# First head of each mixer layer: the first half of the key weights moved between the two halves of the queries, and the last residual's squares put into other PSUM banks

## The chip, the cores and the metric

The kernel runs on one core of a Trainium2 chip. The metric is the device time of one execution in microseconds (us). Everything is computed in float32; the large matmuls run as three float32r products of a high and a low part of each operand.

## The reference, cut to what matters

One block of one kind (sparse attention, an LRU branch, a gated feed-forward) is followed by two layers of another kind. The change touches the start and the end of those two layers and the very end of the program.

```python
def second_block(x, norm1_g, w_in, q_norm_g, k_norm_g, ...):       # x: 1 x 512 x 1024
    for i in range(DEPTH_2):                                       # two layers
        xn = rmsnorm(x, norm1_g[i])
        proj = xn @ w_in[i]
        u_pool, q, k, v, g_a, g_b = jnp.split(proj, splits, axis=-1)
        q = q.reshape(b, s, DIFF_HEADS, 2, DIFF_QK_DIM).transpose(0, 2, 3, 1, 4)   # 4 heads
        k = k.reshape(b, s, DIFF_HEADS, 2, DIFF_QK_DIM).transpose(0, 2, 3, 1, 4)
        q = apply_partial_rotary(rmsnorm(q, q_norm_g[i]), cos, sin)
        k = apply_partial_rotary(rmsnorm(k, k_norm_g[i]), cos, sin)
        ...
        o = diff_attention(q, k, v, lam)
        ...
        x = x + merged @ w_out[i]
        hn = rmsnorm(x, norm2_g[i])
        gate, up = jnp.split(hn @ w_ffn_in[i], 2, axis=-1)
        x = x + (jax.nn.silu(gate) * up) @ w_ffn_out[i]
    return x
```

## The kernel before

x is kept transposed in `xT`, as 8 tiles of 128 channels by 512 tokens. A norm is not applied to x: `residual` writes x times the gain as a high and a low part into `xg`, squares go into PSUM (ScalarE, L2664) and are summed into `acc` (VectorE, L1628), and the projections run on `xg` before the norm's factor is known. The factor is put in later, when the products are read out of PSUM.

Each engine has its own program, in the order in which it is written; engines wait for one another by semaphores. The two mixer layers run in a loop on every engine. Weights come by DMA into four slots, are split into a high part (ScalarE, L3125, or GpSimd, L804) and a low part (VectorE, L2329, or GpSimd, L806) and go to one of three slots for TensorE, in the order of the chunk numbers that `mixer_order` gives out. The first three chunks of a layer are split by GpSimd at the end of the layer ahead.

PSUM has eight banks: `psA` (2), `psB` (5, of which `psS` is the first two and `psT` the other three) and `psO` (1). Projections go through a ring of four banks: `psA[0]`, `psA[1]`, `psT[1]`, `psT[2]`. The queries of a head take the first two of a layer (`TILE2` 0 and 1), its keys the other two.

A head's queries or keys are 256 columns wide and are made by `rows(x, n, j)` (L1471): for one half j of the contraction, 4 slices of 128 channels by 4 token blocks by 3 products, that is 48 matmuls of 128x256. The halves j = 0 and 1 are accumulated in the same banks. TensorE's order at the start of a layer is

- queries half 0, queries half 1 (the last of its slices waits for the last residual tile),
- the norm's sums: a 128x512 matmul with `ones` (L1518), a small one for the layer's lambda (L1520) and four of one column (L1522), which give each token's sum of squares,
- keys half 0, two slices of keys half 1, the transposes of the first half of the tokens of the queries (`rows_transposes`, L1511), the other two slices of keys half 1, half of `u0`, the transposes of the queries' second half, and so on to the values.

Between the sums and the first transposes VectorE makes the token factors (`token_scale`, L2307 to L2313), ScalarE squares the queries with them (`squares2`, L3132), VectorE sums the squares (L2333), ScalarE takes the roots (L3137, L3139), and VectorE applies them and the rotation (`rows_apply`, L2345 to L2363) and starts the norm's own factor (L1633). The first transposes wait for the rotation and, since they write `psO`, for L1633.

At the end of a layer `down_residual` (L2218, L2220) adds the last products to x and calls `residual` for the next layer's norm. After the second layer TensorE transposes x back (L1592), ScalarE copies it out of PSUM (L3292) and sends it to memory, in four blocks of tokens.

Of the kernel before, what the change touches and what calls it, by code (L numbers as in the profile page):

```python
# [17 lines left out]
ALU = mybir.AluOpType  # L18
ACT = mybir.ActivationFunctionType
AX = mybir.AxisListType  # L20

P = 128
# [46 lines left out]
def mixer_order():  # L69

    head = [("q", 0), ("q", 1), ("k", 0), ("k", 1)]
    units = [(x, 0, j) for x, j in head] + [("u", 0), ("u", 1), ("v", 0, 0), ("v", 0, 1)]
    for n in range(HEADS2 - 1):
        units += [(x, n + 1, j) for x, j in head]
        units += [("u", 2 * n + 2), ("p", n), ("u", 2 * n + 3), ("v", n + 1, 0), ("v", n + 1, 1)]
    units += [("g", 0, 0), ("g", 0, 1), ("p", HEADS2 - 1)]
    return units + [("g", m, x) for m in range(1, KT) for x in range(2)]
# [131 lines left out]
def build(nc, a, out):  # L209
    with ExitStack() as ctx:  # L210
# [19 lines left out]
        xT = keep(KT, T)  # L230
# [356 lines left out]
        def _(sp):  # L587
# [157 lines left out]
            with sp.Fori(0, LAYERS) as l:  # L745
                def col2(w, col, k0=0, kts=KT, each=KT):
                    h = kts // 2
                    return [(b, e, w[:, bass.ds(l * each + (k0 + b), e - b), bass.ds(col, P)]) for b, e in ((0, h), (h, kts))]

                c0 = l * C_LAYER + C_B2  # L750
                def head_rows(slot, b):
                    return slot.rearrange("p k n -> p (k n)").rearrange("p (k n) -> p k n", n=V2)[:, 2 * b:2 * b + 2, :]

                def head(x, n, j):
                    c = CHUNK2[x, n, j]
                    col = D * ("uqkv".index(x)) + n * V2
                    load(c0 + c, c % RAW, [(b, 0, wi2[:, bass.ds(l * KT + (4 * j + 2 * b), 2), col:col + V2]) for b in range(2)], head_rows, settle=True)

                def columns(key, col):
                    c = CHUNK2[key]  # L760
                    load(c0 + c, c % RAW, col2(wi2, col), settle=True)

                def pool_weights(g):
                    c = CHUNK2["p", g]
                    load(c0 + c, c % RAW, [(2 * k, 2 * k + 2, pw2[:, bass.ds(l * 8 + (g * 2 + k), 1), :, :].squeeze(1)) for k in range(2)], settle=True)

                def query_key(n):
                    for x in "qk":
                        for j in range(2):
                            head(x, n, j)  # L770

                query_key(0)
                for m in range(2):
                    columns(("u", m), m * P)
                for j in range(2):
                    head("v", 0, j)
                for n in range(HEADS2 - 1):
                    query_key(n + 1)
                    columns(("u", 2 * n + 2), (2 * n + 2) * P)
                    pool_weights(n)  # L780
                    columns(("u", 2 * n + 3), (2 * n + 3) * P)
                    for j in range(2):
                        head("v", n + 1, j)
                for m in range(KT):
                    for x in range(2):
                        columns(("g", m, x), m * P + D * (4 + x))
                    if m == 0:
                        pool_weights(HEADS2 - 1)
                tail(sp, load, stage, c0 + L_WO, lambda: sp.wait_ge(m2_dve.sem, m2_dve.at(l * KT + KT - 1)), lambda m: col2(wo2, m),
                     lambda x, b, q: gate_up2[:, b, bass.ds(l * KT // 2, KT // 2), x * DFF + 2 * q * P:x * DFF + (2 * q + 2) * P],  # L790
                     lambda r, m: col2(wd2, m, r, min(KT, FT - r), FT))
# [412 lines left out]
        def _(pe):  # L1204
# [233 lines left out]
            with pe.Fori(0, LAYERS) as l:  # L1438
# [17 lines left out]
                def rows(x, n, j, kts=range(4), ready=None):  # L1456

                    c, t = CHUNK2[x, n, j], TILE2[x, n]
                    if kts[0] == 0:
                        weights(c)  # L1460
                        if j == 0:
                            take(t)
                            take(t + 1)
                    w = slots2[c % 3]
                    for k in kts:
                        kt = 4 * j + k
                        if ready is not None:
                            ready(kt)
                        for q in range(TT):
                            for m, (xh, wh) in enumerate(((0, 0), (0, 1), (1, 0))):  # L1470
                                i = mm(ring(t + q // 2)[:, q % 2 * V2:(q % 2 + 1) * V2], xg[:, xh, kt, q * P:(q + 1) * P],  # L1471
                                       w[:, wh, k * V2:(k + 1) * V2], start=kt == 0 and q % 2 == 0 and m == 0,
                                       stop=kt == KT - 1 and q % 2 == 1 and m == 2, skip_group_check=True)
                    if kts[-1] == 3:
                        i.then_inc(used.sem, 1)
# [37 lines left out]

                ready = split_by(res_dve, l * 16 + 16)
                rows("q", 0, 0, ready=ready)
                rows("q", 0, 1, ready=ready)
                pe.wait_ge(res_dve.sem, res_dve.at(l * 16 + 23))
                mm(psO[:, :], ones, acc[:, :], start=True, stop=True)  # L1518
# [2 lines left out]
                for t in range(TT):  # L1521
                    i = mm(psT[:, 0, 8 + t:9 + t], acc[:, t * P:(t + 1) * P], ones[:, 0:1], start=True, stop=True)  # L1522
                i.then_inc(nm_pe.sem, 1)
                rows("k", 0, 0)
                rows("k", 0, 1, (0, 1))
                rows_transposes(0, "q", 0)
                rows("k", 0, 1, (2, 3))
# [60 lines left out]
            for t in range(TT):  # L1588
                if t >= 2:
                    pe.wait_ge(ou_act.sem, ou_act.at(t - 2))  # L1590
                for f in range(KT):
                    i = nc.tensor.transpose((psT, psS)[t % 2][:, f // 4, f % 4 * P:(f % 4 + 1) * P], xT[:, f, t * P:(t + 1) * P], ident)  # L1592
                i.then_inc(ou_pe.sem, 1)


# [1 line left out]
        def _(dve):  # L1597
# [14 lines left out]
            def flat(b):  # L1612
                return b[:, :, :, :].rearrange("p h k t -> p h (k t)")

            def residual(n, m, s, gain, add, c=None):

                x = xT[:, :, :].rearrange("p k t -> p (k t)")[:, bass.ds(m * T, T)]
                g2 = flat(xg)
                if add:
                    dve.wait_ge(used.sem, used.at(c))  # L1620
                    v.tensor_tensor(x, x, psA[:, s, :], ALU.add).then_inc(drained.sem, 1)
                dve.wait_ge(res_act.sem, res_act.at(n, "hi"))
                v.scalar_tensor_tensor(g2[:, 1, bass.ds(m * T, T)], x, gain, hi_f(g2[:, 0, bass.ds(m * T, T)]),
                                       ALU.mult, ALU.subtract).then_inc(res_dve.sem, 1)
                if add is False and n:
                    dve.wait_ge(res_dve.sem, res_dve.at(n - 1))
                dve.wait_ge(res_act.sem, res_act.at(n, "square"))
                v.tensor_tensor(acc[:, :], acc[:, :], psT[:, 1 + s, :], ALU.add).then_inc(res_dve.sem, 1)  # L1628

            def norm(k):  # L1630

# [470 lines left out]
            def tail_dve(c0, t0, k, n, of, gain1):  # L2102
# [112 lines left out]
                def down_residual(m):  # L2215
                    s = m % 2
                    dve.wait_ge(used.sem, used.at(c2 + (3 * m + 2)))
                    v.scalar_tensor_tensor(psA[:, s, :], psA[:, s, :], -0.5, c_rs[:, :], ALU.mult, ALU.mult).then_inc(dn_dve.sem, 1)  # L2218
                    dve.wait_ge(dn_dve.sem, dn_dve.at(d0 + m))
                    v.tensor_tensor(xT[:, m, :], xT[:, m, :], psA[:, s, :], ALU.add).then_inc(drained.sem, 1)  # L2220
                    residual(n + 8 + m, m, s, gain1(m), None)

                g, x0, d0, f0, p0 = of(QUADS), of(KT // 2), of(KT), of(QUADS - 1), of(5 * QUADS - 2)
                c2 = c1 + SEVEN * QUADS
# [412 lines left out]
        def _(act):  # L2637
# [18 lines left out]
                act.wait_ge(of.sem, of.at(n, "root"))  # L2656
                ac(n_r2[:, 0:w], n_r0[:, 0:w], ACT.Square, scale=dim ** -0.5).then_inc(of.sem, 1)

            def residual(n, t, m, s, gain):

                x = xT[:, :, :].rearrange("p k t -> p (k t)")[:, bass.ds(m * T, T)]
                act.wait_ge(drained.sem, drained.at(t))
                ac(flat(xg)[:, 0, bass.ds(m * T, T)], x, ACT.Copy, scale=gain).then_inc(res_act.sem, 1)
                ac(psT[:, 1 + s, :], x, ACT.Square).then_inc(res_act.sem, 1)  # L2664

            def norm(k, load=True):
                if load:
# [312 lines left out]
            def tail_act(c0, r0, t0, k, n, g, x0, loads, gain2, gain1):  # L2980
# [128 lines left out]
                for m in range(KT):  # L3109
                    if m < KT - 1:  # L3110
                        down_hi(3 * m + 3)
                        down_hi(3 * m + 4)
                        down_hi(3 * m + 5)
                    residual(n + 8 + m, t0 + 8 + m, m, m % 2, gain1(m))

            tail_act(C_WO, R_WO // RAW, T_WO, 1, 8, 0, 0, lambda q: (q // 2 + 1) * 64, lambda m: col("n2", m), lambda m: par2[:, bass.ds(m + PAR2["n1"].start, 1)])

# [171 lines left out]

            for t in range(TT):  # L3290
                act.wait_ge(ou_pe.sem, ou_pe.at(t))
                ac(yout[:, t, :], (psT, psS)[t % 2][:, 0:2, :].rearrange("p b d -> p (b d)"), ACT.Copy).then_inc(ou_act.sem, 1)  # L3292
                act.wait_ge(ou_act.sem, ou_act.at(t))
                act.dma_start(out[0, t * P:(t + 1) * P, :], yout[:, t, :]).then_inc(stored, 16)
            act.wait_ge(stored, TT * 16)
# [14 lines left out]
```

## Time and profile before

| | us |
|---|---|
| median of 3 runs | 2557.98 |
| lowest and highest run | 2553.32, 2561.17 |
| the profiled execution | 2563.48 |
| its span | 2560.7 |
| TensorE busy in it | 2491.8 (97%) |
| VectorE, ScalarE, GpSimd busy | 1614.1, 1358.4, 710.0 |
| mean granted TensorE clock | 0.984 of full |

A profiled execution is one execution, and all times of single instructions come from it. Its span is the time from the first instruction to the last; 2.8 us of its time lie around the span. A wait of TensorE is a wait of the kernel wherever TensorE has no spare time later, and at 97% it has little.

### The profile page before, as it was taken

The numbers are of one execution on the slowest core, as the hardware profiler recorded it, in microseconds if no ns is written. First come the engines' busy times: TensorE is split into PE (matmuls) and PEld (weight loads), VectorE is DVE, ScalarE is ACT, GpSimd is POOL, SyncE is SP. The second block draws the span as 40 slices with busy tenths as digits, with TensorE's granted clock in tenths as the row PEclk, the third lists the DMA queues.
The fourth block names the chain that finished last, engine by engine and source line by source line (L and its number), as shares of the span: only waits on it lengthen the run. The fifth ranks groups of instructions, "written<-read, shape, count | busy, mean of one in ns | idle before, by whom it ended". The sixth has DMA issues, their size and how long they took to land.

```text
span 2560.7 us, 42520 instructions
## 1 busy us (share of the span) xinstructions
PE 2491.8 (97%) x15323; PEld 2227.9 (87%) x15323; DVE 1614.1 (63%) x2680; ACT 1358.4 (53%) x2001; POOL 710.0 (28%) x373
## 2 busy tenths in 40 slices
PE   7999999999999999999999999999999999999998
PEld 6789988887889998899888899988898888899987
DVE  6567766664575664377775765673577766765653
ACT  4456664764377772244444576652344444667732
POOL 4335530000047760200000177720200000477600
PEclk9989998999999999999999999999999999999999
DMA  7321113333323323322223333333222233233232
GB/s 158 103 53 34 36 34 89 89 85 90 108 81 121 109 79 107 95 71 71 71 79 91 99 100 100 100 99 99 84 76 74 61 89 105 77 104 122 85 99 70
DMA packets 352569, 223.89 MB, mean 87 GB/s; under 512 B 57392, under 2 KB 350572, under 8 KB 352364
## 3 DMA queue, kind: packets, MB, share of 16 engines
q1 hardware_dynamic: 349404, 218.02, 29.2%
q10 hardware_dynamic: 2960, 3.22, 0.4%
q8 instruction: 119, 1.95, 0.3%
q14 instruction: 86, 0.70, 0.1%
HBM read 212.86 MB, written 2.10 MB: 84 GB/s over the span
## 4 chain that ended last, share of the span: by engine, by line
PE 82%; DVE 10%; ACT 4%; issue 3%; DMA 0%; DVEq 0%; ACTq 0%; POOL 0%
PE psA L1215 17%; PE psA L989 13%; PE psB L1238 13%; PE psA L1238 10%; PE psB L989 10%; PE psA L1471 6%; PE psB L1471 5%; PE psO L1116 3%; PE psB L1097 2%; PE psB L1073 1%; DVE b L2329 1%; DVE b L2213 1%; DVE b L2477 1%; DVE b L2159 0%; DVE b L1837 0%
## 5 line engine op out<-in xcount | busy, mean ns | idle before, releaser
L1215 PE MATMUL psA<-b,b 128*128 128x512 f32 x2448 | 568.5, 393 | 2.8 <-DVE b L1657 1.2
L1215 PEld LDWEIGHTS psA<-b,b 128*128 128x128 f32 x2448 | 460.1, 188 | 108.6 <-issue 4.1
L989 PE MATMUL psA<-b,b 128*128 128x256 f32 x3168 | 399.1, 284 | 10.1 <-DVE b L2159 5.0
L989 PEld LDWEIGHTS psA<-b,b 128*128 128x128 f32 x3168 | 387.4, 192 | 14.4 <-issue 8.8
L1238 PE MATMUL psB<-b,b 128*128 128x512 f32 (+4 forms) x1626 | 368.1, 384 | 7.7 <-DVE b L2046 4.5
L916 POOL TENSOR_TENSOR b<-b 128x1024 f32<-128x1024 f32 x33 | 80.6, 2442 | 1036.2 <-DMA b<-in_w_ffn_in 727.9
L1238 PEld LDWEIGHTS psB<-b,b 128*128 128x128 f32 (+2 forms) x1626 | 299.7, 196 | 68.3 <-DVE b L2046 4.9
L1238 PE MATMUL psA<-b,b 128*128 128x512 f32 x1356 | 325.9, 395 | 0.0
L3032 ACT ACTIVATE b<-b 128x1024 fp32r<-128x1024 f32 x231 | 244.2, 1057 | 137.9 <-PE psB L989 76.5
L1238 PEld LDWEIGHTS psA<-b,b 128*128 128x128 f32 x1356 | 253.7, 189 | 54.8 <-issue 1.0
L989 PE MATMUL psB<-b,b 128*128 128x256 f32 x2376 | 299.0, 282 | 0.0
L989 PEld LDWEIGHTS psB<-b,b 128*128 128x128 f32 x2376 | 290.3, 191 | 0.0
L2159 DVE TENSOR_TENSOR b<-psB,b 128x1024 fp32r<-128x1024 f32 x159 | 194.4, 1223 | 113.7 <-ACT psB L3039 113.4
L2145 DVE TENSOR_TENSOR b<-b,b 128x1024 fp32r<-128x1024 f32 x72 | 87.9, 1225 | 149.4 <-ACT b L3018 149.4
L940 POOL TENSOR_TENSOR b<-b,b 128x1024 fp32r<-128x1024 f32 x63 | 154.3, 2449 | 74.7 <-ACT b L3032 64.8
L3039 ACT ACTIVATE psB<-b 128x1024 f32<-128x1024 f32 x159 | 161.2, 1014 | 8.1 <-DVE b L2159 8.0
L3018 ACT ACTIVATE b<-b 128x1024 fp32r<-128x1024 f32 x72 | 76.3, 1059 | 167.2 <-PE psA L1215 164.7
L1471 PE MATMUL psA<-b,b 128*128 128x256 f32 x1152 | 148.6, 288 | 3.2 <-DVE b L2220 3.2
L1471 PEld LDWEIGHTS psA<-b,b 128*128 128x128 f32 x1152 | 143.6, 194 | 6.7 <-issue 6.0
L1471 PE MATMUL psB<-b,b 128*128 128x256 f32 x1152 | 147.8, 288 | 0.6 <-DVE b L2329 0.6
L1471 PEld LDWEIGHTS psB<-b,b 128*128 128x128 f32 x1152 | 143.2, 194 | 2.7 <-issue 2.4
L3125 ACT ACTIVATE b<-b 128x1024 fp32r<-128x1024 f32 x102 | 106.3, 1058 | 56.4 <-PE psA L1238 30.6
(318 smaller groups left out, 3393.8 us busy)
## 6 DMA issues: line engine op xcount, KB each, us to landing
b<-in_w_in SPq DMA_DIRECT2D x296, 256.0 KB, 3.0
b<-in_w_ffn_in SPq DMA_DIRECT2D x88, 512.0 KB, 5.9
b<-in_w_ffn_out SPq DMA_DIRECT2D x64, 256.0 KB, 3.0
b<-in_w_out SPq DMA_DIRECT2D x48, 256.0 KB, 2.9
b<-in_w_gate SPq DMA_DIRECT2D x22, 512.0 KB, 4.9
b<-in_w_up SPq DMA_DIRECT2D x22, 512.0 KB, 6.5
b<-in_w_down SPq DMA_DIRECT2D x32, 256.0 KB, 3.2
b<-in_w_ffn_out SPq DMA_DIRECT2D x32, 192.0 KB, 2.5
```

The lines of the kernel that those rows point to most:

```text
L916: nc.gpsimd.tensor_tensor(sum1[:, :], raw[:, 2, :], raw[:, 3, :], ALU.add).then_inc(sa_pool.sem, 1)
L940: nc.gpsimd.tensor_tensor(w[:, 1], quad_raw(q)[:, {A12: 1, A22: 3}[x]], hi_f(w[:, 0]), ALU.subtract).then_inc(w_lo.sem, 1)
L989: i = nc.tensor.matmul(banks[x][:, p * half_t:(p + 1) * half_t], w[:, wh, at:at + P], rhs[x][:, xh, j, :], start=first and j == 0 and p == ...
L1116: i = mm(psO[:, qt * P:(qt + 1) * P], PT[:, h, at:at + P], vtok[:, br, kt, n // 4, hd, :, :].rearrange("p h d -> p (h d)"), start=h == 0 a ...
L1215: i = mm(dst, w[:, wh, kt * P:(kt + 1) * P], rhs(xh, kt), start=first and kt == 0 and n == 0, stop=last and kt == kts - 1 and n == 2)
L1238: i = mm(dst, lh(x), rh(y), start=start and n == 0, stop=stop and n == 2, skip_group_check=skip)
L1471: i = mm(ring(t + q // 2)[:, q % 2 * V2:(q % 2 + 1) * V2], xg[:, xh, kt, q * P:(q + 1) * P], w[:, wh, k * V2:(k + 1) * V2], start=kt == 0 ...
L2145: v.tensor_tensor(w[:, 1], wraw[:, d % RAW], hi_f(w[:, 0]), ALU.subtract).then_inc(w_lo.sem, 1)
L2159: v.tensor_tensor(w[:, 1], src, hi_f(w[:, 0]), ALU.subtract).then_inc(w_lo.sem, 1)
L3032: ac(quad_slot(c)[:, 0], src[:, :], ACT.Copy).then_inc(w_hi.sem, 1)
L3039: ac(psS[:, :, :].rearrange("p b t -> p (b t)"), src[:, :], ACT.Copy).then_inc(wc_act.sem, 1)
L3125: ac(w[:, 0], wraw[:, c % RAW], ACT.Copy).then_inc(w_hi.sem, 1)
```

## The change

1. The first head's chunks stand in the order queries half 0, keys half 0, queries half 1, keys half 1, in `mixer_order` (chunk numbers, so weights' slots), in the DMA queue's program and in TensorE's program. The heads after the first keep theirs. TensorE makes the norm's sums after queries half 1, as before.
2. Keys half 0 now writes `psT[1]` and `psT[2]` before the last residual's squares have been read. So the last residual of a layer puts its squares into `psS`. The other residuals stay.
3. The squares of the second layer's last residual now lie in `psS` when x is transposed back, so the odd token blocks of the output go through `psA` in place of `psS`.

```diff
     head = [("q", 0), ("q", 1), ("k", 0), ("k", 1)]
-    units = [(x, 0, j) for x, j in head] + [("u", 0), ("u", 1), ("v", 0, 0), ("v", 0, 1)]
+    units = [("q", 0, 0), ("k", 0, 0), ("q", 0, 1), ("k", 0, 1)] + [("u", 0), ("u", 1), ("v", 0, 0), ("v", 0, 1)]
...
-                query_key(0)
+                for j in range(2):
+                    for x in "qk":
+                        head(x, 0, j)
...
                 rows("q", 0, 0, ready=ready)
+                rows("k", 0, 0)
                 rows("q", 0, 1, ready=ready)
                 pe.wait_ge(res_dve.sem, res_dve.at(l * 16 + 23))
                 mm(psO[:, :], ones, acc[:, :], start=True, stop=True)
...
                 i.then_inc(nm_pe.sem, 1)
-                rows("k", 0, 0)
                 rows("k", 0, 1, (0, 1))
                 rows_transposes(0, "q", 0)
...
-                    i = nc.tensor.transpose((psT, psS)[t % 2][:, f // 4, f % 4 * P:(f % 4 + 1) * P], xT[:, f, t * P:(t + 1) * P], ident)
+                    i = nc.tensor.transpose((psT, psA)[t % 2][:, f // 4, f % 4 * P:(f % 4 + 1) * P], xT[:, f, t * P:(t + 1) * P], ident)
...
-            def residual(n, m, s, gain, add, c=None):
+            def residual(n, m, s, gain, add, c=None, squares=psT[:, 1:3, :]):
...
-                v.tensor_tensor(acc[:, :], acc[:, :], psT[:, 1 + s, :], ALU.add).then_inc(res_dve.sem, 1)
+                v.tensor_tensor(acc[:, :], acc[:, :], squares[:, s, :], ALU.add).then_inc(res_dve.sem, 1)
...
-                    residual(n + 8 + m, m, s, gain1(m), None)
+                    residual(n + 8 + m, m, s, gain1(m), None, squares=psS)
...
-                ac(psT[:, 1 + s, :], x, ACT.Square).then_inc(res_act.sem, 1)
+                ac(squares[:, s, :], x, ACT.Square).then_inc(res_act.sem, 1)
...
-                    residual(n + 8 + m, t0 + 8 + m, m, m % 2, gain1(m))
+                    residual(n + 8 + m, t0 + 8 + m, m, m % 2, gain1(m), squares=psS)
...
-                ac(yout[:, t, :], (psT, psS)[t % 2][:, 0:2, :].rearrange("p b d -> p (b d)"), ACT.Copy).then_inc(ou_act.sem, 1)
+                ac(yout[:, t, :], (psT, psA)[t % 2][:, 0:2, :].rearrange("p b d -> p (b d)"), ACT.Copy).then_inc(ou_act.sem, 1)
```

TensorE's program at the start of a mixer layer, before. `wsp` is b3, the third weight slot is b71, `xg` is b4, `ones` lies in b5, `acc` is b11. The rows are queries half 0, half 1, the sums, and keys half 0.

```order
L1471 MATMUL psA<-b71_119,b4_52 128x256 x47
L1471 MATMUL psA<-b3_51,b4_52 128x256 [waits weights_lo]
L1471 MATMUL psA<-b3_51,b4_52 128x256 x35
L1471 MATMUL psA<-b3_51,b4_52 128x256 [waits residual_vector]
L1471 MATMUL psA<-b3_51,b4_52 128x256 x11
L1518 MATMUL psO<-b11_59,b5_53 128x512 [waits residual_vector]
L1520 MATMUL psB<-b16_64,b5_53 128x2 [waits layer_vector]
L1522 MATMUL psB<-b5_53,b11_59 128x1 x4
L1471 MATMUL psB<-b3_51,b4_52 128x256 x47
L1471 MATMUL psB<-b71_119,b4_52 128x256 x23
L1506 ISA [waits query_key_rows]
L1511 MATMUL psO<-b5_53,b81_129 128x128 [waits norm_vector]
```

The same place of the changed kernel (its lines stand two or three further down).

```order
L1473 MATMUL psA<-b71_119,b4_52 128x256 x47
L1473 MATMUL psB<-b3_51,b4_52 128x256 x47
L1473 MATMUL psA<-b3_51,b4_52 128x256 [waits weights_lo]
L1473 MATMUL psA<-b3_51,b4_52 128x256 x35
L1473 MATMUL psA<-b3_51,b4_52 128x256 [waits residual_vector]
L1473 MATMUL psA<-b3_51,b4_52 128x256 x11
L1521 MATMUL psO<-b11_59,b5_53 128x512 [waits residual_vector]
L1523 MATMUL psB<-b16_64,b5_53 128x2 [waits layer_vector]
L1525 MATMUL psB<-b5_53,b11_59 128x1 x4
L1473 MATMUL psB<-b71_119,b4_52 128x256 x23
L1508 ISA [waits query_key_rows]
L1513 MATMUL psO<-b5_53,b81_129 128x128 [waits norm_vector]
```

The 48 matmuls of keys half 0, which stood behind the sums, stand ahead of queries half 1. Between the sums and the first transposes 72 matmuls stood before, and 24 now.

ScalarE's program between the sums and the first transposes is, in both kernels, the token roots, the squares of the queries, the high part of the weights of `u0`, the roots of the queries. In the kernel before:

```order
L3192 ACTIVATE b_133<-b_133 128x4 [waits token_scale]
L3194 ACTIVATE b_133<-b_133 128x4 [waits token_roots]
L3132 ACTIVATE b_60<-psA,b_133 128x256 [waits chunk_used]
L3132 ACTIVATE b_60<-psA,b_133 128x256 x3
L3125 ACTIVATE b_51<-b_50 128x1024 [waits chunk_used,weights_loaded0]
L3137 ACTIVATE b_132<-b_132,b_64 128x4 [waits query_key_sums]
```

And in the changed one:

```order
L3194 ACTIVATE b_133<-b_133 128x4 [waits token_scale]
L3196 ACTIVATE b_133<-b_133 128x4 [waits token_roots]
L3134 ACTIVATE b_60<-psA,b_133 128x256 [waits chunk_used,token_scale]
L3134 ACTIVATE b_60<-psA,b_133 128x256 x3
L3127 ACTIVATE b_51<-b_50 128x1024 [waits chunk_used]
L3139 ACTIVATE b_132<-b_132,b_64 128x4 [waits query_key_sums]
```

Nothing moved there but where a wait is attached. VectorE's, GpSimd's and the DMA queue's programs keep their order too; the DMA queue's second and third load of a layer fetch other columns of the same size.

## Rows read from the trace of the kernel before

**Rows 1.** The page, busy us: share of the span and instructions of each engine.

```profile
PE 2491.8 (97%) x15323; PEld 2227.9 (87%) x15323; DVE 1614.1 (63%) x2680; ACT 1358.4 (53%) x2001; POOL 710.0 (28%) x373
```

**Rows 2.** TensorE's waits: us in total, times, longest us.

```profile
PE psO L1511 <- DVE b L2369: 11.4, 6, 2.7
...
PE psA L1471 <- DVE b L2220: 3.2, 2, 1.6
...
PE psB L1471 <- DVE b L2329: 0.6, 2, 0.3
```

**Rows 3.** The chain that ended last, in time, first layer: start, us, what.

```profile
1075.10 11.77 PE psA L1471 x96
1086.86 0.86 PE psO L1518 x2
1087.84 0.91 PE psB L1522 x8
1088.97 0.21 ACT b L3192
...
1096.63 0.70 DVE b L1633
...
1111.84 1.14 DVE b L2329
1112.99 0.21 issue
1113.20 6.02 PE psB L1471 x48
```

**Rows 4.** Timeline of TensorE: start, us, instructions [idle before <-releaser]; both layers.

```profile
1088.60 8.87 PE L1471 MATMUL psB<-b,b 128*128 128x256 f32 x72
1097.38 0.66 PE L1511 MATMUL psO<-b,b 128*128 128x128 f32 x4
1097.79 3.13 PE L1471 MATMUL psB<-b,b 128*128 128x256 f32 x24
1100.76 2.93 PE L1238 MATMUL psA<-b,b 128*128 128x512 f32 x12
...
1826.06 8.87 PE L1471 MATMUL psB<-b,b 128*128 128x256 f32 x72
1834.83 0.65 PE L1511 MATMUL psO<-b,b 128*128 128x128 f32 x4
```

**Rows 5.** Timeline of VectorE, ScalarE and GpSimd at the first layer's start.

```profile
1075.88 2.85 POOL L806 TENSOR_TENSOR b<-b,b 128x1024 fp32r<-128x1024 f32 x1
...
1076.40 0.68 DVE L1628 TENSOR_TENSOR b<-b,psB 128x512 f32<-128x512 f32 x1
...
1088.77 0.16 DVE L2307 TENSOR_SCALAR b<-psB 128x4 f32<-128x4 f32 x1 [5.31 <-PE psB L1522]
...
1096.63 0.68 DVE L1633 SCALAR_TENSOR_TENSOR b<-psO,b 128x512 f32<-128x512 f32 x1
```

**Rows 6.** Timeline of TensorE elsewhere: gaps, and what 48 matmuls took behind them.

```profile
587.69 11.24 PE L1238 MATMUL psA<-b,b 128*128 128x512 f32 x48
603.46 13.90 PE L1238 MATMUL psB<-b,b 128*128 128x512 f32 x48 [4.53 <-DVE b L2046]
...
1173.90 6.02 PE L1471 MATMUL psA<-b,b 128*128 128x256 f32 x48
...
1236.13 0.63 PE L1511 MATMUL psO<-b,b 128*128 128x128 f32 x4 [1.93 <-DVE b L2369]
1236.70 7.51 PE L1471 MATMUL psB<-b,b 128*128 128x256 f32 x48
```

**Rows 7.** Busy us of engines by stretch, then PEclk (granted clock), DMA share, GB/s.

```profile
605.00:610.00 5.00, 5.00 (x16) 3.92 (x15) 0.00 (x0) 0.07 (x1) 0.00 (x0) 0.61 0.01 3
...
1120.00:1140.00 20.00, 20.00 (x162) 19.74 (x161) 12.60 (x31) 9.32 (x23) 0.00 (x0) 1.00 0.32 93
...
1236.00:1239.00 3.00, 2.87 (x15) 2.72 (x16) 3.00 (x4) 1.09 (x2) 0.00 (x0) 0.66 0.09 31
```

**Rows 8.** Timeline around the output's start: TensorE and ScalarE.

```profile
2550.63 1.97 PE L1592 MATMUL psB<-b,b 128*128 128x128 f32 x16 [1.52 <-DVE b L2220]
2551.24 0.58 ACT L2664 ACTIVATE psB<-b 128x512 f32<-128x512 f32 x1
...
2552.84 1.09 PE L1592 MATMUL psB<-b,b 128*128 128x128 f32 x8 [0.24 <-ACT b L3292]
```

More of the change, by code:

```diff
@@ L2657, in roots, with residual @@
                 ac(n_r2[:, 0:w], n_r0[:, 0:w], ACT.Square, scale=dim ** -0.5).then_inc(of.sem, 1)
-            def residual(n, t, m, s, gain):
+            def residual(n, t, m, s, gain, squares=psT[:, 1:3, :]):
                 x = xT[:, :, :].rearrange("p k t -> p (k t)")[:, bass.ds(m * T, T)]
```

## The prediction, as it was put on record

> **What bounds the kernel now.** I read the page first: TensorE is busy 97% of the span, VectorE 63%, ScalarE 53% [rows 1]. So a change counts by what it does to TensorE's waits and to nothing else. The second view is the list of TensorE's waits, cut to the lines near the change: the queries' first half waits 1.6 us a layer for the last residual tile to be drained, the values' weights make it wait 0.3 us a layer, and six waits for the low part of rotated queries or keys make 11.4 us in all [rows 2]. None of them stands in front of the queries' second half, which the change moves. The third view, the chain that ended last in order of time, says more than the waits do. From 1075.10 to the sums' end it is TensorE. Then it leaves TensorE and runs over VectorE and ScalarE from the token sums (1087.84) to the weights of the values (1111.84 + 1.14), and comes back to TensorE only at 1113.20 [rows 3]. So in these 24.6 us, from 1088.60 to 1113.20, the small operations behind the sums are the bound, and TensorE's matmuls there are their cover. They fit nearly exactly: 72 matmuls begin at 1088.60 and the first transposes stand behind them at 1097.38 [rows 4], and the operation that releases these transposes, L1633 on VectorE, runs from 1096.63 for 0.68 us, to 1097.31 [rows 5]. In the second layer it is the same to 0.01 us: 1826.06 and 1834.83 [rows 4].
>
> **Part 1: keys half 0 moves ahead of queries half 1.** The sums need only the last residual and stand behind the queries by program order. 48 matmuls now go in front of them. Their cost is taken from the stretch itself: the 24 matmuls that begin at 1097.79 are followed by the next at 1100.76, so 24 take 2.97 us [rows 4]; the 72 take 8.78 us (1088.60 to 1097.38), which leaves 5.81 us for the 48 that move. The sums come 5.81 us later in each layer. Whether this is paid depends on what the time behind the sums is made of. All that VectorE and ScalarE do from the sums to L1633 is anchored there: VectorE had waited 5.31 us for the token sums when L2307 began at 1088.77 [rows 5], and the order on both engines is unchanged. From the place behind the sums to the first transposes this takes 8.78 us, as before. TensorE has 24 matmuls for it in place of 72, 2.97 us. So it waits 8.78 - 2.97 = **5.81 us** at the transposes, a wait that wasn't there. From then on TensorE and the other two engines stand to each other as before, all 5.81 us late, and at the values' half 0 nothing is won back, since that was waited for by the chain too. The matmuls that move are not saved anywhere: the total of TensorE's work is the same.
>
> **What the clock adds.** The new wait is long. Where TensorE waited 1.93 us, the granted clock then fell (0.66 in 1236 to 1239 [rows 7]; of the levels 2.4 and 1.2 GHz that is a mixture) and 48 matmuls took 7.51 us, against 6.02 us for the same 48 at 1173.90: 1.49 us lost. Where it waited 4.53 us, the clock was 0.61 in 605 to 610 [rows 7], and 48 matmuls took 13.90 against 11.24 us: 2.66 us lost [rows 6]. Behind the 1.6 us wait ahead of the queries nothing was lost (96 in 11.77 us, no slower than the rest [rows 3]). For a wait of 5.8 us the bounds are 0, as behind the shortest, and 2.9 us, which is the loss if the clock stays at half for as long as the wait was. I take the middle of the two that fell, (1.49 + 2.66) / 2 = 2.08 us, since with a longer wait more of the slow time falls into the wait itself. Of this the 0.3 us are absorbed in which TensorE waits for the values' weights anyway [rows 2]: 1.78 us a layer.
>
> **Part 2: squares in `psS`, output through `psA`.** ScalarE's square takes 0.58 us into one bank [rows 8] and writes as many bytes to the other; the weights' copies that used `psS` are read before the down products. The residual's sum was at its end at 1077.08 [rows 5], and queries half 1 needs it for its last slice only, 84 matmuls behind 1075.10, which is about 1085.4 at 11.77 / 96 us each: it had 8.3 us in hand, and has 14 now. The output's transposes wait 1.52 us for the last drain, and the third and fourth block for ScalarE's copy (0.24 us [rows 8]), whichever bank they use. I cost all of this at nothing; bounds are plus or minus 0.3 us, that 0.24 us gap doubled or gone. A wait for weights is not added either: chunks 1 and 2 are both split by GpSimd, and its last operation of the three chunks begins at 1075.88 and takes 2.85 us [rows 5], before the queries' first half is over (48 matmuls from 1075.10).
>
> **The sum.** 2 layers x (5.81 + 1.78) = 15.2 us. The profiled execution took 2563.48 us and would take 2578.7. It was 5.5 us slower than the median of the runs, 2557.98, so the median goes to **2573.2 us**, 0.6% slower. From no change a measurement of this kernel can tell about 0.3%, 7.7 us.
>
> What the row shows is that keys half 0 was the cover of the queries' evacuation [rows 3, 4]. The Trainium skill (Perfetto Trace Analysis, Optimizing Tensor Performance, Matmuls) has the rule that independent groups of matmuls should rotate through banks so that one group's evacuation overlaps the next group's matmuls. By it the new order is the worse one too, since of one and a half chunks that ran under the queries' evacuation half a chunk is left. It names no price, and a sum by it would be the 5.8 us of a moved chunk in each layer and nothing for the clock.
>
> **Rivals.**
> (a) The wait alone, with no loss to the clock. What speaks for it is the 1.6 us wait without loss. Against it are both longer ones. 2 x (5.81 - 0.3) = 11.0, so 2569 us.
> (b) More than the sum. If each gap costs 2.9 us of slow clock and a later wait of the same layer, that takes no slow clock now, grows and takes 1.5 us of it, as the 1.9 us wait did [rows 6], 2 x (5.81 + 2.9 + 1.5) = 20.4, so 2578 us. For it: six waits for L2369 stand in these layers [rows 2].
> (c) Given back later. The six waits for L2369 make 5.7 us a layer. If VectorE carries a backlog through the layer, TensorE's delay eats into them, down to nothing at best: 15.2 - 11.4 = 3.8, so 2562 us. Against it: VectorE was busy 12.60 of 20 us in 1120 to 1140 [rows 7], so it has no backlog and waits for TensorE in its turn.
> (d) Not slower. L1633 ends 0.07 us before the transposes begin, but no record shows TensorE waiting there. If the operations behind the sums were held up by TensorE's 72 matmuls themselves (by sharing PSUM, say) and went faster without them, the chain would shrink. It decides at 2.97 us: as long as it takes less than that, nothing is lost, and the 0.3 us waits of both layers go, 2557 us. Against it: it would have to shrink from 8.78 to a third, and VectorE's and ScalarE's operations stand nearly back to back in it. The Trainium skill (Perfetto Trace Analysis, Matmul Optimizations) asks that all eight PSUM banks be used so that instructions can overlap, by which four open banks at once would be no loss, as in this case. I see no row that would let TensorE gain by it.
> (e) The order doesn't change what I think it does, or something speeds up that I don't see.
>
> **How the numbers follow.** Forecast 0.66, (a) 0.13, (b) 0.09, (c) 0.06, (d) 0.04, (e) 0.02. The forecast, (a) and (b) are slower by over 0.3%: 0.88. (c) and (d) are within: 0.10. (e) I give to faster: 0.02. The forecast's own spread is the clock, 0 to 2.9 us a layer, so 2569 to 2575, and the median of a few runs moves by some 4 us (the three runs span 7.8). The range that leaves out (c), (d) and (e) and part of (b) is 2564 to 2579 us.
>
> **What would show it.** Right: in both layers a wait of TensorE of about 5.8 us in front of the first transposes of a layer (L1513 in the changed file), released by VectorE's L1635 (L1633 before), at 8.7 to 8.9 us behind the sums; the granted clock under 1.00 behind it; the values' half 0 some 24.6 to 26.5 us behind the sums; nothing else moved. Wrong: 24 matmuls followed by the transposes without a wait (then d), the same wait but shorter waits for L2369 in the three heads behind (then c), no drop of the clock (a), or new waits in front of the queries' second half.

## The result, and the profile after

| | kernel before | changed kernel |
|---|---|---|
| median, us | 2557.98 (5 runs) | 2573.72 (5 runs) |
| lowest and highest, us | 2553.32, 2561.17 | 2569.68, 2576.76 |
| the profiled execution, its span, us | 2563.48, 2560.7 | 2575.04, 2572.5 |
| TensorE busy, us | 2491.8 | 2494.2 |

The changed kernel is slower: the ratio is 1.0061, with a 95% interval of 1.0045 to 1.0078. In a second session, beside 15 runs of the kernel before (median 2560.18), it took 2573.03 us, a ratio of 1.0054 (1.0041 to 1.0068).

The list of TensorE's waits of the changed kernel (us in total, times, longest) has one new entry of weight. The others that answer to [rows 2] are as they were; that for the values' weights (0.6 us, 2 times) has gone.

```profile
PE psO L1513 <- DVE b L2371: 11.4, 6, 2.7
PE psO L1513 <- DVE b L1635: 11.1, 2, 5.6
...
PE psA L1473 <- DVE b L2222: 3.2, 2, 1.6
```

L1513 is the transposes (L1511 before), L1635 the first step of the norm's factor (L1633 before). The timeline of TensorE at the start of the first layer shows where it lies; the columns are start, duration, instructions and, in brackets, the idle time before them and what ended it. It answers to [rows 4].

```profile
1076.29 6.01 PE L1473 MATMUL psA<-b,b 128*128 128x256 f32 x48 [1.62 <-DVE b L2222]
1082.14 5.92 PE L1473 MATMUL psB<-b,b 128*128 128x256 f32 x48
1087.90 5.92 PE L1473 MATMUL psA<-b,b 128*128 128x256 f32 x48
1093.66 1.02 PE L1521 MATMUL psO<-b,b 128*128 128x512 f32 x2
...
1095.55 3.13 PE L1473 MATMUL psB<-b,b 128*128 128x256 f32 x24
1104.24 1.12 PE L1513 MATMUL psO<-b,b 128*128 128x128 f32 x4 [5.56 <-DVE b L1635]
1105.00 4.17 PE L1473 MATMUL psB<-b,b 128*128 128x256 f32 x24
1109.02 2.90 PE L1240 MATMUL psA<-b,b 128*128 128x512 f32 x12
...
1120.88 5.93 PE L1473 MATMUL psB<-b,b 128*128 128x256 f32 x48
```

The first 48 are queries half 0, then keys half 0 (into `psB`, which holds `psT`), queries half 1 and the sums. The 24 behind the sums are all that is left in front of the transposes. The 24 behind the transposes took 4.17 us; the same 24 took 3.13 us before [rows 4]. The chain that ended last, in order of time, tells the same from the other side (start, us, what):

```profile
1094.80 0.91 PE psB L1525 x8
1095.73 0.17 DVE b L2309
...
1103.50 0.69 DVE b L1635
1104.19 0.04 issue
1104.24 1.12 PE psO L1513 x4
1105.35 3.83 PE psB L1473 x24
1109.18 2.74 PE psA L1240 x12
```

As in [rows 3] it leaves TensorE at the token sums. But where it stayed on VectorE and ScalarE until the values' first half, it is back on TensorE at the first transposes and stays there.

Cut at three landmarks, the layer starts compare like this. The first is the start of queries half 0, the second the matmul that follows the sums, the third the first transposes, the fourth the values' first half.

| us | before, layer 1 and 2 | changed, layer 1 and 2 |
|---|---|---|
| queries half 0 to behind the sums | 13.50, 13.49 | 19.26, 19.26 |
| from there to the first transposes | 8.78, 8.77 | 8.69, 8.68 |
| from there to the values' first half | 15.82, 15.83 | 16.64, 16.87 |
| together | 38.10, 38.09 | 44.59, 44.81 |

That is 6.49 and 6.72 us, 13.2 us in all. (The starts of layer 2 are 1812.57, 1826.06, 1834.83, 1850.66 us before and 1819.83, 1839.09, 1847.77, 1864.64 us in the changed kernel.) The two spans are 11.8 us apart; what is between 13.2 and 11.8 comes and goes outside the layer starts (the first of them already stood 1.2 us later), as it does from one execution of one kernel to the next.

### The profile page after: what moved, and what is told of

The parts are those of the page before. It is cut to its first block, busy times and chain, and to the rows that moved or that the text cites. A ratio compares the mean times of both kernels' runs of the same rounds, so it can differ in the third digit from the quotient of the medians.

```text
span 2572.5 us, 42520 instructions
## 1 busy us (share of the span) xinstructions
PE 2494.2 (97%) x15323; PEld 2231.4 (87%) x15323; DVE 1612.4 (63%) x2680; ACT 1358.4 (53%) x2001; POOL 710.5 (28%) x373
## 4 chain that ended last, share of the span: by engine, by line
PE 83%; DVE 9%; ACT 4%; issue 3%; DMA 0%; DVEq 0%; ACTq 0%; POOL 0%
PE psA L1217 17%; PE psA L991 13%; PE psB L1240 13%; PE psA L1240 11%; PE psB L991 10%; PE psA L1473 6%; PE psB L1473 5%; PE psO L1118 3%; PE psB L1099 2%; PE psB L1075 1%; PE psO L1513 1%; DVE b L2161 1%; DVE b L2215 1%; DVE b L2479 1%; DVE b L2331 0%
```

## The experiments

The first four ran in one session, the last four in a second one on another chip, each beside the kernel before (median 2560.18 us in the first, 2559.03 us in the second). They are compared with that median alone. "The layer start" is the distance from queries half 0 to the values' first half: 38.1 us before, 44.6 and 44.8 us in the changed kernel.

### The changed kernel again

> The changed kernel once more, beside the others on the same chip. My theory counts the two layer starts as 6.5 and 6.7 us longer in the profiled execution, 13.2 us together, so it expects 2571 us where the kernel before gives 2558; the medians of the first measurement are 15.7 us apart. If more than 15 us show again, something outside the two layer starts is dearer too.

Measured: 2573.03 us against 2560.18 us, 12.9 us apart. The layer starts took 44.58 and 44.73 us. So the 15.7 us of the first measurement were partly its own scatter; the two layer starts, 13.1 us, are enough to account for the loss.

### The banks alone

> Only the banks change (last squares in psS, odd output blocks through psA); the order of the first head's chunks is that of the kernel before. My theory: nothing, 2558 us, within 2 us, the values' first half 38.1 us behind the queries' first half as before. Rival: the banks cost the part of the 15.7 us that the layer starts don't show (2.5 us), 2560.5 us.

```diff
-    units = [("q", 0, 0), ("k", 0, 0), ("q", 0, 1), ("k", 0, 1)] + [("u", 0), ...
+    units = [(x, 0, j) for x, j in head] + [("u", 0), ...
...
                 rows("q", 0, 0, ready=ready)
-                rows("k", 0, 0)
                 rows("q", 0, 1, ready=ready)
...
+                rows("k", 0, 0)
                 rows("k", 0, 1, (0, 1))
```

(against the changed kernel; the DMA queue's order goes back with it). Measured: 2559.38 us in 11 runs, ratio 0.9998 (0.9988 to 1.0009). In its timeline queries half 0 starts at 1071.23 and the values' half 0 at 1109.33 us, 38.10 us. The second layer's takes 38.11 us. The squares in `psS` and the output through `psA` cost nothing that can be measured (the interval is -3 to +2 us), and the loss is the order's.

### The wait filled with work

> The changed kernel with 44 extra matmuls of 128x256 into the free bank psS[0] ahead of the first transposes, so that TensorE works (about 5.3 us) where it waited 5.56 us; their result is not used. If the wait costs its own length and, on top, a slow clock behind it, the slow clock goes: the stretch from the transposes to the values' first half falls from 16.64 and 16.87 us back to 15.8, and the time to 2558 + 11.4 = 2569.4 us. Rival: the slow stretch has nothing to do with the wait, and the time stays at that of the changed kernel or rises if the extra matmuls hold up VectorE and ScalarE.

```diff
                 rows("k", 0, 1, (0, 1))
+                for _ in range(44):
+                    mm(psS[:, 0, 0:V2], xg[:, 0, 1, 0:P], xg[:, 0, 0, 0:V2], start=True, stop=True, skip_group_check=True)
                 rows_transposes(0, "q", 0)
```

TensorE's timeline in this kernel, first layer:

```profile
1087.54 3.13 PE L1473 MATMUL psB<-b,b 128*128 128x256 f32 x24
1090.51 5.43 PE L1529 MATMUL psB<-b 128*128 128x256 f32 x44
1096.24 0.66 PE L1513 MATMUL psO<-b,b 128*128 128x128 f32 x4 [0.30 <-DVE b L1637]
1096.66 3.13 PE L1473 MATMUL psB<-b,b 128*128 128x256 f32 x24
...
1112.06 6.01 PE L1473 MATMUL psB<-b,b 128*128 128x256 f32 x48 [0.27 <-DVE b L2333]
```

The transposes come 8.70 us behind the sums, as with an idle TensorE (8.69 us): the 44 matmuls neither hold up the chain nor help it. Behind them the 24 take 3.13 us again, and the stretch to the values' first half is 15.82 and 15.84 us, as in the kernel before. The busy times and the granted clock by stretch (the last columns are the granted clock, the DMA share and GB/s) say why:

```profile
1090.00:1096.00 6.00, 5.94 (x50) 5.74 (x48) 4.77 (x15) 4.14 (x9) 0.00 (x0) 1.00 0.23 78
1096.00:1100.00 4.00, 3.76 (x30) 3.72 (x31) 2.94 (x9) 1.53 (x4) 0.00 (x0) 1.00 0.06 16
```

and in the changed kernel, at the same place:

```profile
1099.00:1100.00 1.00, 0.00 (x0) 0.00 (x0) 0.07 (x2) 1.00 (x2) 0.00 (x0) 1.00 0.00 0
1100.00:1101.00 1.00, 0.00 (x0) 0.00 (x0) 1.00 (x1) 0.94 (x4) 0.00 (x0) 0.78 0.00 0
...
1104.00:1105.00 1.00, 0.76 (x4) 0.77 (x5) 0.91 (x3) 0.00 (x0) 0.00 (x0) 0.50 0.30 91
...
1106.00:1107.00 1.00, 1.00 (x6) 1.00 (x6) 0.40 (x2) 0.54 (x3) 0.00 (x0) 0.50 0.00 0
1107.00:1108.00 1.00, 1.00 (x9) 1.00 (x8) 0.90 (x5) 1.00 (x2) 0.00 (x0) 0.81 0.00 0
```

The clock fell to 0.50, the 1.2 GHz level, within the wait and came back between 1107 and 1108 us, 3 us after work began again. With work in the wait it stays at 1.00. So the slow stretch is the wait's own: 0.82 and 1.04 us of the layer starts. The time was 2572.0 us in five runs, ratio 1.0045 (1.0031 to 1.0058), 11.8 us over the kernel before, where 11.4 us were expected. The median can't tell this from the changed kernel itself, 12.9 us over; the timeline can.

The execution in this timeline is the fastest of the five, 2562.87 us, 9 us under their median. It isn't faster in the layer starts, which took 43.78 and 43.80 us, 11.4 us over the kernel before together, as expected. It was ahead already when queries half 0 of the first layer began (1068.28 us, against 1071.70 and 1076.29 us in the two profiles of the changed kernel). That the clock stays up there is seen in both layers of this one execution. For the five only the mean granted clock is on record, 0.984 to 0.990, where the changed kernel's five in the same session had 0.982 to 0.985.

### The transposes later

> The changed kernel, but the first transposes stand behind all of keys half 1 and the first half of u0, so that 8.8 us of matmuls lie between the sums and them, as in the kernel before. Theory A (the whole chain from the sums to the values' weights, 24.6 us, is the bound): the wait goes from the first transposes and comes up at the second ones, about 5.5 us, and the time stays near 2571 to 2574 us. Theory B (only the cover in front of the first transposes matters): the wait goes and the time is that of the kernel before, 2558 us.

```diff
-                rows("k", 0, 1, (0, 1))
-                rows_transposes(0, "q", 0)
-                rows("k", 0, 1, (2, 3))
+                rows("k", 0, 1)
                 columns(("u", 0), range(4))
+                rows_transposes(0, "q", 0)
```

TensorE's timeline, first layer:

```profile
1090.83 6.01 PE L1473 MATMUL psB<-b,b 128*128 128x256 f32 x48
1097.94 3.02 PE L1240 MATMUL psA<-b,b 128*128 128x512 f32 x12 [1.11 <-DVEq L2355]
1100.80 0.60 PE L1513 MATMUL psO<-b,b 128*128 128x128 f32 x4
1105.60 1.02 PE L1513 MATMUL psO<-b,b 128*128 128x128 f32 x4 [4.20 <-DVE b L2370]
```

The first transposes wait for nothing. A wait of 1.11 us stands ahead of `u0`, whose bank is free only when the queries' first half has been applied, and one of 4.20 us at the second transposes. Together 5.31 us, where one of 5.56 us stood. The expectation had all of it at the second transposes and didn't see the one ahead of `u0`. The layer starts took 44.77 and 44.76 us, and the time was 2572.42 us, ratio 1.0049 (1.0035 to 1.0063). Theory A holds and theory B falls. The wait of TensorE can be moved about in the stretch, and it isn't paid by where it stands: what is short is the total of matmuls between the sums and the values.

### Half of the move

> Banks as in the changed kernel, chunk order as before the change, but two of the four slices of keys half 0 (24 matmuls) stand ahead of queries half 1 and the other two behind the sums: half of the move. If the loss is what is taken from under the chain, the sums come 2.9 us later, the first transposes wait 8.7 - 5.9 = 2.8 us, and the values' first half stands 38.1 + 2.9 = 41.0 us behind the queries' first half, up to 41.9 with the slow clock behind the wait (1.5 us less 0.6 us in hand); the time is 5.8 to 7.6 us over the kernel before. Rival: there is a threshold (a wait short enough for the clock costs nothing, or the slack is larger than I think), and the time is within 2 us of the kernel before.

```diff
                 rows("q", 0, 0, ready=ready)
+                rows("k", 0, 0, (0, 1))
                 rows("q", 0, 1, ready=ready)
...
-                rows("k", 0, 0)
+                rows("k", 0, 0, (2, 3))
                 rows("k", 0, 1, (0, 1))
```

(against the kernel with the banks alone). TensorE's timeline, first layer:

```profile
1084.82 5.99 PE L1471 MATMUL psB<-b,b 128*128 128x256 f32 x48
1093.59 1.12 PE L1511 MATMUL psO<-b,b 128*128 128x128 f32 x4 [2.79 <-DVE b L1634]
1094.36 3.99 PE L1471 MATMUL psB<-b,b 128*128 128x256 f32 x24
```

The transposes come 8.77 us behind the sums, and the wait is 2.79 us, where 2.8 was expected. The layer starts took 41.58 and 41.91 us. The time was 2566.28 us against 2559.03, 7.3 us more, ratio 1.0030 (1.0021 to 1.0040). So half the move isn't free: it costs half the wait, and a little over half of the time, since the clock takes about three quarters as much behind a wait of 2.8 us (0.6 and 0.7 us of the layer starts) as behind one of 5.6 (0.8 and 1.0). Whether a still smaller part of the move would be free wasn't run.

### The sums earlier, in the changed kernel

> The changed kernel with the norm's sums and the lambda's sum between keys half 0 and queries half 1, in place of behind queries half 1. The token factors are then ready when the queries are, so the chain behind the queries is shorter by 1.65 us (the sums' 1.9 us of matmuls are out of it, and the squares start at once). The chain theory expects the wait at the first transposes to shrink from 5.56 to about 3.9 us, and the layer start from 44.6 to 42.9 us or less: 3.3 us less in all than the changed kernel. Rival: the chain is paced by something behind the squares (ScalarE's weights copy for u0, say) and the wait stays 5.5 us.

```diff
                 rows("q", 0, 0, ready=ready)
                 rows("k", 0, 0)
+                pe.wait_ge(res_dve.sem, res_dve.at(l * 16 + 23))
+                mm(psO[:, :], ones, acc[:, :], start=True, stop=True)
...
                 rows("q", 0, 1, ready=ready)
-                pe.wait_ge(res_dve.sem, res_dve.at(l * 16 + 23))
-                mm(psO[:, :], ones, acc[:, :], start=True, stop=True)
...
```

```profile
1090.44 3.04 PE L1473 MATMUL psB<-b,b 128*128 128x256 f32 x24
1097.55 1.12 PE L1513 MATMUL psO<-b,b 128*128 128x128 f32 x4 [4.07 <-DVE b L1635]
1098.32 5.08 PE L1473 MATMUL psB<-b,b 128*128 128x256 f32 x24
```

The wait shrank from 5.56 to 4.07 us, about as the chain theory had it. But the 24 matmuls behind it took 5.08 us, against 4.17. The granted clock stayed at 0.50 until here:

```profile
1096.00:1097.00 1.00, 0.00 (x0) 0.00 (x0) 0.96 (x5) 0.00 (x0) 0.00 (x0) 0.50 0.88 284
...
1102.00:1103.00 1.00, 1.00 (x7) 1.00 (x7) 0.96 (x5) 0.00 (x0) 0.00 (x0) 0.62 0.00 0
```

which is 5 us of work at the slow level, where the longer wait had 3 us. The layer starts took 44.00 and 43.91 us, 0.6 and 0.9 us less than in the changed kernel, not 1.7 or more. The time was 2571.84 us, 12.8 us over the kernel before, as the changed kernel's was in its session. The expectation missed: the wait was predicted rightly, and its shortening was given back at the slow clock.

### Queries half 0 bank by bank, in the kernel before

> The kernel before, with the queries' first half in another order: all matmuls that write psA[0] first, then those of psA[1], so that only the second 24 wait for the last residual tile to be drained. TensorE waited 1.62 us there in each layer. If that wait is worth its length, the time is 3.2 us less than before's, and the sums' chain, being anchored to TensorE, comes as much earlier. Rival: the last residual tile, which queries half 1 needs for its last slice, or GpSimd's weights hold the queries up instead, and it is worth nothing.

```diff
-                rows("q", 0, 0, ready=ready)
+                rows("q", 0, 0, ready=ready, blocks=(0, 1), last=False)
+                rows("q", 0, 0, ready=ready, blocks=(2, 3))
...
                         if j == 0:
                             take(t)
-                            take(t + 1)
+                            if blocks[0] == 0 and len(blocks) == 4:
+                                take(t + 1)
+                    if blocks[0] == 2 and j == 0:
+                        take(t + 1)
...
-                        for q in range(TT):
+                        for q in blocks:
```

Measured: 2556.53 us in 12 runs, ratio 0.9989 (0.9979 to 0.9999), 2.5 us less than the kernel before, where 3.2 were expected. In the first layer the wait for the last drain is gone. In the second a wait of 1.01 us stands in its place, so 2.2 us of waits went:

```profile
1808.09 11.99 PE L1474 MATMUL psA<-b,b 128*128 128x256 f32 x96 [1.01 <-POOL b L806]
```

What is named there is GpSimd's split of the second chunk, over at 1807.55 us. Queries half 0 doesn't wait for it: in the first layer it began at 1070.43, before that split was over at 1071.06 us. So it was something else, which the wait for the drain had covered. Its cause is open. One thing differs between the layers: one transfer of an instruction queue (q8) begins between 1805.0 and 1805.5 us and one between 1808.0 and 1808.5 us, about the start at 1808.09, while none begins between 1066 and 1071 us. No run tests whether they matter. The interval reaches to 0.9999, so the gain is only just told from none.

### Both, in the kernel before

> The kernel before with both: the queries' first half bank by bank, and the sums between the two halves of the queries. The chain behind the queries' second half is 1.65 us shorter and no longer the bound of the stretch, so the waits of 0.3 us at the third transposes and at the values go as well. Expected: 3.2 + 1.2 = 4.4 us less than before's, 0.17%, about what the interval can tell. Rival: 0, if what TensorE gains is waited for elsewhere in the layer.

The edit is that of the last experiment, and the sums' lines stand between the two halves of the queries. TensorE's timeline, first layer:

```profile
1084.31 8.80 PE L1474 MATMUL psB<-b,b 128*128 128x256 f32 x72
1092.95 0.60 PE L1514 MATMUL psO<-b,b 128*128 128x128 f32 x4
...
1108.13 5.93 PE L1474 MATMUL psB<-b,b 128*128 128x256 f32 x48
```

The wait at the values is gone; at the third transposes neither kernel's list shows one, but they come 0.11 us sooner. The layer starts took 37.30 and 37.68 us, against 38.1. Measured: 2555.41 us in 12 runs, ratio 0.9984 (0.9973 to 0.9995), 3.6 us less than the kernel before, where 4.4 were expected. The 1.01 us wait of the last experiment is there again in the second layer (its queries half 0 begins at 1806.49 us), and it is about what is missing from the 4.4. Of all versions this one's interval lies clearest under 1. How much of the 3.6 us belongs to the sums alone the times can't say, since the intervals of the last two experiments overlap; in the timelines the layer starts with the sums late took 37.99 and 38.30 us, so the sums are worth 1.3 us, where 1.2 was expected.

## Why the prediction was right, point by point

**The time.** 2573.2 us was predicted, 2573.72 us measured; the loss of 15.2 us was 15.7 in the first session and 12.9 in the second, and 13.2 in the two layer starts of the profiled executions. So the predicted loss is 2 us too high, and that the first median agrees to 0.5 us is luck.

**What bounds the stretch.** That the operations behind the sums are a chain of fixed length was the step on which all rested. It measured 8.78 us with 72 matmuls beside it, 8.77 with 48, 8.69 with 24 and 8.70 with 24 and 44 others. The 0.09 us aren't rival (d), since the chain with 68 matmuls beside it is as short as the one with 24. They lie at one place: ScalarE's squares begin 1.75 us behind VectorE's first step in the kernels with the chunk order of before (1088.77 to 1090.52 us in the kernel before, the same with the banks alone and with half the move), and 1.66 or 1.67 us behind it in those with the changed order, the filled one too. So they go with the order of the chunks and not with TensorE's load. That order also moved the wait attached to ScalarE's squares; that this is the reason is likely and not shown.

**The wait.** 5.81 us was predicted, 5.56 and 5.55 us measured. Most of the difference, 0.16 us, is in how the cover is counted: 24 matmuls were taken as 2.97 us, from one start to the next, while the profile counts them busy to their modelled end, 3.13 us. The rest is the chain's 0.09 us. What the sums moved by was 5.76 and 5.77 us, against 5.81.

**The clock.** This is the term of the sum that was mis-sized: 1.78 us a layer was put in, 0.82 and 1.04 us were paid. The clock fell, as predicted, and against rival (a). It took 1.40 us in layer 1 and 1.64 us in layer 2 over the transposes and the 24 matmuls behind them (4.78 and 5.02 us, against 3.38 us before), where 2.08 us was put in. And more of it was absorbed than the 0.3 us put in: from the second transposes to the values' first half it took 9.12 us in the changed kernel (1111.76 to 1120.88) against 9.68 us before (1103.52 to 1113.20), so TensorE had 0.56 us in hand there, of which the list of waits shows only 0.3 us. Over the two layers that is 1.7 us of the 2. The reason given for taking the middle, that a longer wait holds more of the slow time in itself, isn't borne out as a rule: over the transposes and the 24 matmuls the wait of 5.56 us lost less than the one of 4.07 us (2.31 and 2.24 us), but the one of 2.79 us lost less than both (1.21 and 1.32 us). No single row gives the size.

The Trainium skill (TensorE: Matmul & The Clock Gate, What's actually happening) puts it that throttled is the array's resting state, and that activity releases it. The trace agrees, if not at once: the granted clock stayed at 1.00 for the first 1.9 us of the wait, then stood at 0.50 to 3 us into the work behind it, and was 1.00 throughout when the wait was filled.

**The banks and the output** cost nothing, as predicted (0.9998). **Given back later** (c) didn't happen: the six waits for the low parts are 11.4 us in both kernels, wait by wait. **Not slower** (d) and **the larger loss** (b) are out as well: the 5.6 us wait is there, and no later wait of the layers grew.

## What to carry to other kernels

Where the chain that ended last leaves the busiest engine and runs over others for a while, that engine's work in the stretch is cover. Here all of it was needed: moving 48 matmuls from behind the chain's start to ahead of it made each layer longer by nearly their whole length (5.7 of 5.8 us) and about 1 us of slow clock, though no work was added and TensorE had been waiting almost nowhere. Count what each side of the chain's anchor holds before an instruction is carried across it, and look for what can be carried the other way (here the anchor itself, the sums). A wait that opens on TensorE also has a price in clock behind it, and shortening the wait doesn't shorten that price in step; work that filled it did away with it, in the one execution profiled.

## What the runs showed of the hardware that was not expected

A shorter wait can lose more than a longer one. Behind the wait of 5.56 us the 24 matmuls took 4.17 us, behind 4.07 us they took 5.08 us, behind 2.79 us 3.99 us, and 3.13 us with no wait. All three waits ended with the granted clock at 0.50. It is the slow work behind a wait that counts, and by these rows it doesn't grow with the wait.

The rows show where it comes from: from when the clock falls in the wait and when it comes back. Around the wait of 5.56 us it stood at 0.50 from 1100.6 to 1107.4 us, 3.1 us of it behind the start of the transposes; around 4.07 us from 1095.9 to 1102.7 us, 5.2 us of it; around 2.79 us from 1092.9 to 1096.3 us, 2.8 us of it. And the same wait of the same kernel isn't met by the same fall. In the second session's profile of the changed kernel TensorE waited 5.57 us in the first layer, from 1094.09 to 1099.66 us, and the clock fell only at its end (here too the last columns are the granted clock, the DMA share and GB/s):

```profile
1098.00:1099.00 1.00, 0.00 (x0) 0.00 (x0) 0.85 (x5) 0.00 (x0) 0.00 (x0) 1.00 0.83 279
1099.00:1100.00 1.00, 0.34 (x2) 0.34 (x3) 0.96 (x3) 0.00 (x0) 0.00 (x0) 0.66 0.68 229
```

In its second layer it fell 2.2 us into a wait of 5.56 us. So one profile of each version doesn't order the waits by what they cost. What decides when the clock falls the runs don't show.
